# Sixteen query and key/value blocks multiplied by quarters of the features during the first conditioning of a hybrid decoder layer

## What is computed

```python
# conditioning: 6 x 2048 values for each of 9 sequences, from c (9 x 2048)
shift, scale, gate, ... = silu(c) @ w_ada + b_ada
h = x * (1 + scale) + shift
proj = h @ w_in + b_in
q, kvc, kvs, kvw, nsa_g, r_x, r_y, merge_g = split(proj)
```

## Time and profile before

| | |
|---|---|
| times of the kernel | 1776.35, 1777.85, 1779.82 us; median 1777.85 |
| span of the profiled execution, first to last instruction | 1777.5 us |
| that execution's own time | not listed apart; the span lies 0.35 us below the median |
| PE busy | 1741.4 us, 98% |
| PE weight loads | 1607.3 us, 90% |
| DVE, ACT, POOL busy | 899.4, 710.7, 156.7 us |
| DMA | 384.06 MB, 216 GB/s in the mean |
| mean granted clock of TensorE | 0.989 |

### The profile page before, as it was taken

The page is one execution under the profiler, slowest core; times in us unless marked ns, Lnnn a source line. Parts: engine busy times, 40 slices in busy tenths (PEclk is TensorE's granted clock), DMA queues, the critical chain, the costliest instruction groups (busy, mean ns, idle before and its releaser), DMA issues.

```text
span 1777.5 us, 34633 instructions
## 1 busy us (share of the span) xinstructions
PE 1741.4 (98%) x13610; PEld 1607.3 (90%) x13610; DVE 899.4 (51%) x1632; ACT 710.7 (40%) x1076; POOL 156.7 (9%) x271
## 2 busy tenths in 40 slices
PE   8989999999999999999999999999999999999997
PEld 3558879888999999889988899999999999999997
DVE  2233346655656555555874344444444444444565
ACT  2223227764445443343563343333333333333334
POOL 0001312213322311100000000000000000000001
PEclk9999999999999999999999999999999999999998
DMA  9998878866655647985647764444455454544552
GB/s 354 380 380 308 295 245 296 286 213 236 200 178 171 205 148 278 334 315 193 200 142 264 284 223 165 159 135 163 162 185 185 157 167 160 167 151 142 166 164 85
DMA packets 114152, 384.06 MB, mean 216 GB/s; under 512 B 14941, under 2 KB 15325, under 8 KB 113662
## 3 DMA queue, kind: packets, MB, share of 16 engines
q1 hardware_dynamic: 103248, 349.82, 56.9%
q0 software_dynamic: 10208, 32.32, 5.6%
q10 hardware_dynamic: 590, 0.44, 0.1%
HBM read 373.48 MB, written 9.03 MB: 215 GB/s over the span
## 4 chain that ended last, share of the span: by engine, by line
PE 90%; DMA 5%; ACT 1%; DVE 1%; issue 1%; SPq 0%; POOL 0%; POOLq 0%; ACTq 0%; DVEq 0%
PE bank L714 26%; PE bank L716 25%; PE bank L715 25%; DMA raw<-in_w_units 5%; PE bank L721 3%; PE bank L761 3%; PE bank L739 2%; PE bank L887 1%; PE bank L1010 1%; DVE wlo L377 1%; PE bank L923 1%; DMA mgate<-mg 0%; SPq L478 0%; ACT z L1511 0%; PE bank L954 0%
## 5 line engine op out<-in xcount | busy, mean ns | idle before, releaser
L714 PE MATMUL bank<-xhi,wlo 128*128 128x288 f32 x2544 | 758.5, 298 | 2.4 <-DVE wlo L377 1.7
L715 PE MATMUL bank<-xlo,whi 128*128 128x288 f32 x2544 | 750.5, 295 | 0.0
L716 PE MATMUL bank<-xhi,whi 128*128 128x288 f32 x2544 | 748.1, 294 | 0.0
L377 DVE TENSOR_TENSOR wlo<-raw,whi 128x1024 fp32r<-128x1024 f32 (+2 forms) x468 | 510.0, 1127 | 380.5 <-ACT whi L369 373.3
L369 ACT CAST whi<-raw 128x1024 fp32r<-128x1024 f32 (+2 forms) x468 | 434.2, 969 | 421.1 <-PE bank L716 273.4
L714 PEld LDWEIGHTS bank<-xhi,wlo 128*128 128x128 f32 x2544 | 476.7, 187 | 15.7 <-issue 13.8
L716 PEld LDWEIGHTS bank<-xhi,whi 128*128 128x128 f32 x2544 | 479.1, 188 | 0.0
L715 PEld LDWEIGHTS bank<-xlo,whi 128*128 128x128 f32 x2544 | 477.7, 188 | 0.6
L716 PE MATMUL bank<-hhi,whi 128*128 128x288 f32 x704 | 208.7, 296 | 0.0
L714 PE MATMUL bank<-hhi,wlo 128*128 128x288 f32 x704 | 208.3, 296 | 0.0
L715 PE MATMUL bank<-hlo,whi 128*128 128x288 f32 x704 | 205.3, 292 | 0.0
(11 more groups left out here) (332 smaller groups left out, 1686.7 us busy)
## 6 DMA issues: line engine op xcount, KB each, us to landing
raw<-in_w_units SPq DMA_DIRECT2D x556, 512.0 KB, 6.1
raw<-in_w_ffn_out_units SPq DMA_DIRECT2D x64, 384.0 KB, 3.0
raw<-in_w_ffn_out_units SPq DMA_DIRECT2D x64, 320.0 KB, 3.4
raw<-in_w_units SPq DMA_DIRECT2D x16, 448.0 KB, 8.5
mgate<-mg POOLq DMA_DIRECT2D x32, 144.0 KB, 3.9
mgl<-mgate POOLq DMA_DIRECT2D x16, 288.0 KB, 7.0
bz<-relrow POOLq DMA_DIRECT2D x16, 192.0 KB, 3.5
xt<-in_x SPq DMA_DIRECT2D x8, 288.0 KB, 7.3
```

Source lines behind the costliest of these rows:

```text
L377: nc.vector.tensor_tensor(wlo[e][:, part], raw[:, s, spot], f32(whi[e][:, part]), ALU.subtract).then_inc(raw_used[s][h], 1)
L714: pe.matmul(acc, wt[1][:, w], x[0][:, c, :], start=start, stop=False)
L715: pe.matmul(acc, wt[0][:, w], x[1][:, c, :], start=False, stop=False)
L716: return pe.matmul(acc, wt[0][:, w], x[0][:, c, :], start=False, stop=stop)
```

## The change

INIT now has 16 G units instead of 8, and covers 16 column blocks: the eight of q and the first eight of key/value. Unit n holds four column blocks (u = 4 (n mod 4) to + 3) for a quarter of the features (kq = n div 4, four chunks): four parts of 4 x 3 = 12 products. A part is summed in one of seven banks in turn. DVE reads each of the 64 parts out: the first quarter's with the bias into `qT` or `kvT`, the others added to what stands there in SBUF. The first eight A units come ahead of the first G unit, then two per G unit; the last four G units of INIT are each followed by two A units of the gate group. What is left for the stage KVS is the gate unit and four key/value blocks, with two A units between each pair. QS is gone. POOL's waits move with the counter: w1d after unit 12, the pages of sequence b after unit 13 + b.

```diff
-INIT = Stage("AAAAG" * 7 + "GAAAA", 1, 0, 0, 0)
-EARLY = 7
-QS = Stage("AAGGAA", 1, INIT.r_end, INIT.g_end, INIT.a_end)
-KVS = Stage("GGAAGGAA", 3, QS.r_end, QS.g_end, QS.a_end)
+LEAD, QUART, BLOCKS = 8, 4, 16
+INIT = Stage("A" * LEAD + "AAG" * 12 + "GAA" * 4, 1, 0, 0, 0)
+KVS = Stage("GAAGAAGAAGAAG", 1, INIT.r_end, INIT.g_end, INIT.a_end)
...
+        def piece(n, f):
+            m = n * QUART + f
+            return bank[EARLY_BANK[m % 7]][:, 0:T], m
...
             for pos in range(INIT.U):
-                if pos in INIT.A:
...
+                if pos in INIT.A[3:2 * DC:4]:
+                    q = INIT.A.index(pos) // 4
                     sp.dma_start(xt[:, 2 * q:2 * q + 2, :], a["x"][:, 2 * q:2 * q + 2, :]).then_inc(x_in[q % 2], 16)
-                    load(INIT, 0, pos)
...
+                load(INIT, 0, pos, first=pos < RAW_SLOTS)
...
-            pool.wait_ge(unit_done, QS.g0 + 2)
+            pool.wait_ge(unit_done, KVS.g0 - 4)
             pool.dma_start(w1d[:], a["cmp_w1"][0]).then_inc(w1_in[0], 16)
             for b in range(DEC_B):
-                pool.wait_ge(unit_done, KVS.g0 + b)
+                pool.wait_ge(unit_done, KVS.g0 - 3 + b)
                 load_pages(0, b)
-            read_out(pool, QS.g0, 0, 2, 0)
+            read_out(pool, KVS.g0, 0, 5, 0)
...
+            def early_unit(n, fs):
+                s, k = INIT.rawG(0, n)
+                kq = n // 4
+                whole = n % 4 == 0
+                for kks in (((0, 1), (2, 3)) if whole else ((0, 1, 2, 3),)):
+                    for f in fs:
+                        acc, m = piece(n, f)
+                        if kks[0] == 0:
+                            pe.wait_ge(raw_used[s][f // 2], k + 1)
+                            if m >= 7:
+                                pe.wait_ge(part_ok, m - 6)
+                        if whole and f == 0:
+                            pe.wait_ge(mod_lo, 2 * kq + kks[0] // 2 + 1)
+                        for kk in kks:
+                            w = slice((f * QUART + kk) * P, (f * QUART + kk + 1) * P)
+                            ins = step(acc, (whi[n % 2], wlo[n % 2]), w, X, kq * QUART + kk, kk == 0, kk == QUART - 1)
+                        if kks[-1] == QUART - 1:
+                            ins.then_inc(*((part_mm, 1) if f < QUART - 1 else (unit_done, 1)))
...
+            for n in range(12):
+                u = LEAD + 2 * n
+                if u % 4 == 0:
+                    pe.wait_ge(ada_out, u // 4)
+                a_units(INIT, 0, (u, u + 1))
+                if n % 2:
+                    early_unit(n, (0, 1))
+                    a_turn(u // 4)
+                    early_unit(n, (2, 3))
+                else:
+                    early_unit(n, range(QUART))
+            for n in range(12, 16):
+                early_unit(n, range(QUART))
+                for u in range(2 * DC + 2 * n - 24, 2 * DC + 2 * n - 22):
+                    a_part(INIT, 0, u)
...
+            for j in range(5):
+                plain(KVS, 0, j)
+                if j < 4:
+                    a_part(KVS, 0, 2 * j)
+                    a_part(KVS, 0, 2 * j + 1)
+            kv_written(pe)
+            read_out(pe, KVS.g0, 0, 5, 0)
...
+            for n in range(15):
+                q = (LEAD + 2 * n) // 4
+                turned = n % 2 == 1 and n < 12
+                if turned:
+                    a_copy(INIT, 0, q)
+                split_hi(act, INIT, 0, n + 1)
+                if turned:
+                    mod_high(0, xm, q, q % 2)
...
+                if u < NP_ and kq == 0:
+                    ins = v.tensor_scalar(dst, acc, qb[:, u:u + 1], SCALE, ALU.add, ALU.mult)
+                elif u < NP_:
+                    ins = v.scalar_tensor_tensor(dst, acc, SCALE, dst, ALU.mult, ALU.add)
+                elif kq == 0:
+                    ins = v.tensor_scalar(dst, acc, kvb[:, (u - NP_) // 4, (u - NP_) % 4:(u - NP_) % 4 + 1], None, ALU.add)
+                else:
+                    ins = v.tensor_tensor(dst, acc, dst, ALU.add)
...
+            for n in range(16):
+                q = (LEAD + 2 * n) // 4
+                turned = n % 2 == 1 and n < 12
+                part_out(n, 0)
+                part_out(n, 1)
+                if turned:
+                    modulated(q)
+                split_lo(dve, *((INIT, 0, n + 1) if n < 15 else (KVS, 0, 0)))
+                part_out(n, 2)
+                if turned:
+                    mod_low(0, xm, q, q % 2)
+                part_out(n, 3)
```

More of the change, by code:

```diff
@@ L481, in _ @@
             for pos in range(INIT.U):
[L482 to L485 removed]
+                if pos in INIT.A[3:2 * DC:4]:
+                    q = INIT.A.index(pos) // 4
                     sp.dma_start(xt[:, 2 * q:2 * q + 2, :], a["x"][:, 2 * q:2 * q + 2, :]).then_inc(x_in[q % 2], 16)
[L487 to L488 removed]
+                load(INIT, 0, pos, first=pos < RAW_SLOTS)
+            for st_ in (KVS, RNN, MRG, CMB, OUT, FIRST, NEXT, FIN[0], FOUT[0], FIN[1], FOUT[1]):
                 if st_.n == 1:
@@ L823, in _ @@
             a_turn(0)
[L824 to L837, removed]
+            pe.wait_ge(ada_out, 1)
+            a_units(INIT, 0, (4, 5, 6, 7))
+            a_turn(1)
+            pe.wait_ge(bias_ok, 1)
+            for n in range(12):
[13 more added lines that the diff above has]
+                    a_part(INIT, 0, u)
             def plain(st_, i, j, ready=None):
@@ L1598, in _, with modulated @@
             v.tensor_copy(biasCS[:], bank[3][:, 0:NCMP]).then_inc(bias_ok, 1)
-            for q in range(8):
-                if q == 7:
-                    split_lo(dve, INIT, 0, q, EARLY * 2 * P)
+            def modulated(q):
                 a_out(q)
@@ L1620, in _, with part_out @@
-            split_lo(dve, QS, 0, 1)
-            split_lo(dve, KVS, 0, 0)
-            dve.wait_ge(unit_done, QS.g0 + 2)
-            v.tensor_scalar(qT[:, EARLY, :], bank[1][:, 0:T], qb[:, EARLY:EARLY + 1], SCALE, ALU.add, ALU.mult).then_inc(acc_free[1], 1)
-            with dve.Fori(0, KVS.n) as i:
-                for j in range(4):
-                    b = (KVS.g0 + j) % 2
-                    split_lo(dve, KVS, i, j + 1)
-                    dve.wait_ge(unit_done, KVS.g(i, j) + 1)
-                    v.tensor_scalar(kvT[:, bass.ds(i, 1), j, :].squeeze(1), bank[b][:, 0:T], kvb[:, bass.ds(i, 1), j],
-                                    None, ALU.add).then_inc(acc_free[b], 1)
+            def part_out(n, f):
+                acc, m = piece(n, f)
+                kq, u = n // 4, (n % 4) * QUART + f
+                if f < QUART - 1:
+                    dve.wait_ge(part_mm, n * (QUART - 1) + f + 1)
+                else:
+                    dve.wait_ge(unit_done, n + 1)
+                dst = qT[:, u, :] if u < NP_ else kvT[:, (u - NP_) // 4, (u - NP_) % 4, :]
+                if kq > 0:
+                    dve.wait_ge(part_ok, m - BLOCKS + 1)
+                if u < NP_ and kq == 0:
[4 more added lines that the diff above has]
+                    ins = v.tensor_scalar(dst, acc, kvb[:, (u - NP_) // 4, (u - NP_) % 4:(u - NP_) % 4 + 1], None, ALU.add)
+                else:
+                    ins = v.tensor_tensor(dst, acc, dst, ALU.add)
+                if m < 57:
+                    ins.then_inc(part_ok, 1)
+                elif m in (57, 63):
+                    ins.then_inc(acc_free[1 if m == 57 else 0], INIT.g_end // 2)
@@ new lines, in _ @@
+            for q in range(2):
+                modulated(q)
+                mod_low(0, xm, q, q % 2)
+            split_lo(dve, INIT, 0, 0)
+            dve.wait_ge(b_in, SMALL)
+            v.tensor_scalar(btanh[:], btanh[:], 0.5, None, ALU.mult)
+            softplus()
+            for n in range(16):
[4 more added lines that the diff above has]
+                if turned:
+                    modulated(q)
+                split_lo(dve, *((INIT, 0, n + 1) if n < 15 else (KVS, 0, 0)))
[3 more added lines that the diff above has]
+                part_out(n, 3)
@@ L1631, in _ @@
+            for j in range(5):
+                b = (KVS.g0 + j) % 2
+                split_lo(dve, KVS, 0, j + 1)
+                if j > 0:
+                    dve.wait_ge(unit_done, KVS.g(0, j) + 1)
+                    v.tensor_scalar(kvT[:, 2, j - 1, :], bank[b][:, 0:T], kvb[:, 2, j - 1:j], None, ALU.add).then_inc(acc_free[b], 1)
             dve.wait_ge(gate_t, 1)
```

83 lines of the change are left out of this document (18 added, 65 removed).

## The result

The changed kernel takes **1790.9 us** (median of five runs, 1787.05 to 1798.56); the kernel before takes 1778.54 (1776.35 to 1779.82). The ratio is 1.0064, with a 95% interval of 1.0046 to 1.0082. The forecast was 1763.2 and faster. The medians lie 12.4 us apart.

The account below looks back on a forecast made before the run. PE was taken to idle some 27 us in the DMA-bound start. PE's and DMA's sums (217.6, 216.7; 221.4 with losses) gave E = 220; cmp_pos 14.2 later starts the compression at 234.2, 14.7 earlier: 1763.2 us, range 1754 to 1773.

Parts of the forecast that it names:

- the DMA sum: Loads after 36.4 us until the last K/V unit: 174.8 us, landed at 211.2; with 5.5 us behind, the stage ends at 216.7.
- E: End of the last K/V unit, before the first compression; forecast at 220 us.
- a sign of being wrong: In the profile after: the last K/V unit ending later than 226 us would show the prediction wrong.
- PE's side: PE's work from 38.6 us to the last K/V unit sums to 179.0 us, ending at 217.6 if PE never waits.
- Rival (b): DMA holds the whole stage at 350 GB/s: -4 us, 1774; chance 0.15 shared with another rival, for gains over 3.6 us.
- Its second figure: Same DMA-bound rival at the skill's 358 GB/s: last K/V unit ends at 229, time 1772 us.
- Rival (c): G loads wait for A units' shared raw slots: cycle 11.15 instead of 9.0 us, about 1806 us, slower; chance 0.07.
- The first product of unit 0: Start of the first G unit on PE, after ten A units' loads: forecast 37.6 us.
- The slow begin: First G unit starting at the lower 1.2 GHz clock after the lead-in: 1.0 us charged, bounds 0 and 3.3.
- The added work on DVE: 68 evacuations and additions from PSUM instead of 20, at 0.51 us each: hidden behind PE, costing nothing.
- POOL's chain: Gate copy, stores and loads before cmp_pos: 22.5 us from trigger to landing, a new 5.1 us wait before the first compression.
- Nothing later changes: After the first compression's start, work and time stay as before, so its 14.7 us gain reaches the end.

## Why the prediction was wrong, point by point

**The step that failed is the rate of the DMA sum.** It read "58 more units of 1.049 MB at 411 GB/s". Measured were 339 to 348 until 190 us and 325 after. The 66.1 MB of that sum take 161 us at 411. At the rates measured window by window they take 194, land at 230.5 and give E = 236, where the DMA sum had 216.7; E was 239.5, past the 226 that the prediction had named as a sign of being wrong. From PE's side, 217.6 plus 15.9 and 4.7 us of waits, plus 2.1 us for a slow stretch behind the longer one (below), is 240.3.

Why 411 was the wrong row: it came from the lead-in, where PE takes the A units as they land, and was carried into a stretch in which SP waits for PE. The row nearest to that was the 376 GB/s at a share of 1.00 in the earlier trace rows, and a working pattern of release that the change makes coarser. I took the difference between 376 and 411 for x slices and small loads, and charged it to them: 1.8 us for an x slice whose 0.29 MB take 0.7 at 411. Part of it was the issue of loads, and that part grew with the change.

**Rival (b) had the size** (350 GB/s), and the side was wrong all the same: at 350 it gave E = 231. The measured rate was lower still, and E later by 8.5. Its argument for itself, the pages, was not the cause. Its second figure was worked out wrongly: at 358 GB/s the 66.1 MB take 185 us, and by (b)'s own steps E is 226.5 and the time 1769.6, not 229 and 1772. The Trainium skill, DMA: Bandwidth & Descriptors, "Where 436 GB/s comes from", puts the HBM side near 358 GB/s; the 344 look like it, but no run here bears it out as a bound, since the same units from the same memory came at 408 to 411 for 80 us and more.

**Rival (c) had the mechanism**: "The load of G unit n+1 can be issued only when PE has used the second A unit before unit n, because they share a raw slot". Its landing of 8.5 us is what the chain shows, 7.7 to 10.2. It turns slower than before when the landing passes some 7.5, by its own text (7.1 to 7.25 by its own terms: 9.0 + 14.7 / 20, or 9.0 + 0.9, less 2.65), and it was: from 60 to 95 us the median from issue to landing is 7.8. The cycle became 9.7 (the pairs of A units at 45.37 and 229.25 stand 19 units apart), not 11.15, and the time 1790.9, not 1806: the landings were shorter than 8.5, and PE waited for wlo twelve times, 2.7 us at most, not in every unit by 2.15. I put 0.07 on it because "the latency is a queue of earlier loads that pass at full rate". They do not: at one unit left in the queue they pass at 316 to 329.

**Right steps.** The first product of unit 0 started at 37.44 (forecast 37.6). The slow begin showed 12 products in 3.05 us, which take 1.6 at the upper level of 2.4 GHz: 1.4 us (forecast 1.0, bounds 0 to 3.3). What ran before it was not as foreseen: the clock of the lead-in is 1.00 this time, where it was 0.51 in the earlier trace rows, and it fell only at about 37, when PE had stood idle since 34.8 us ahead of unit 0. The row of the stretch mixes the two levels:

```profile
37.00:41.00 4.00, 3.56 (x16) 3.56 (x17) 3.42 (x14) 1.82 (x3) 0.00 (x0) 0.57 1.04 408
```

The added work on DVE cost nothing, and its price was right; the in-place addition (L1625, and L1629 for key/value) is a little under the 0.51 assumed (mean ns after the bar):

```profile
L1625 DVE SCALAR_TENSOR_TENSOR qT<-bank,qT 128x288 f32<-128x288 f32 x24 | 10.4, 454 | 10.3 <-PE bank L716 10.2
```

POOL's chain was as worked out. Its timeline answers to the earlier trace rows:

```profile
230.52 0.70 POOL L539 DMA_DIRECT2D cmp_rows<-in_cmp_k  x1 [7.63 <-issue]
...
242.19 6.34 POOL L569 DMA_DIRECT2D gs<-gscr  x12 [6.02 <-DMA gscr<-gTs]
248.53 0.57 POOL L544 DMA_DIRECT2D cmp_rows<-in_cmp_pos  x1
```

From the trigger at 230.0 to the landing at 252.36 are 22.4 us (forecast 22.5), and the wait is 3.9 us (forecast 5.1, bounds 2 to 8).

**The ledger.** The compression was forecast for 234.2 and came at 252.56, 18.4 us late: E is 19.5 us later, and the stretch from E to it took 13.1 instead of 14.2. Within E lies a second slow stretch that the sum had not: late in the 4.7 us wait of the gate unit and behind it the granted clock was 0.51, the 1.2 GHz level, and the 21 products from 192.75 to 197.62 took 4.9 us instead of 2.8:

```profile
190.80:197.60 6.80, 4.86 (x20) 4.86 (x21) 1.89 (x3) 0.63 (x1) 0.00 (x0) 0.51 1.02 400
```

The compression's products took 1.5 us longer than before (the engine had waited before them, and without the wait they took 8.42). Some 2.7 more came behind it: weight waits past 262 us are 4.7 us (20.6 in the whole span less 15.9) against 2.1 before. Together that is the 22.6 between 1785.4 and the forecast span of 1762.8. "Nothing later changes" was thus off by about 3 us; which slot or queue hands that on was not tested. Nor is it settled what makes the changed kernel's runs spread so widely.

## What to carry to other kernels

A transfer rate belongs to a pattern of issue: before carrying one from one stretch into another, look at what frees the buffers, and at how many loads are still outstanding when the next go out. With an in-order queue, two buffers that come free together at the end of a long step block all loads behind them, even those whose own buffers are free; use such buffers early or in the middle of the step. And when overlap makes an engine the bound, its late releases become the transfers' bound, so a sum "the later of the two" is too kind to both.

## What the runs showed of the hardware that was not expected

- Units of 1 MB in two halves of 512 KB, a half issued as one lands: 409 to 410 GB/s with two or four units outstanding, 278 with three halves, 235 with one unit. In bursts of two, 410 with two units left and 329 with one; in bursts of three, 316 to 322 with one left and 281 with none.
- The share of the DMA engines hardly shows it: 0.90 to 0.95 goes with 316 to 329 GB/s and 0.97 with 346. Rate over share is what falls (410 / 1.03 = 398 against 346 / 0.97 = 357).
- Products, casts, subtractions and conditioning products beside the loads cost them nothing: 409 to 411 GB/s in each case, casts and subtractions out of the slots included.
